# A two-layer hybrid encoder on one core: the latent attention's combine reads PSUM, three TensorE regroupings, the third chunk's weights rounded earlier

## The reference, cut to what matters

```python
def _layer(x, ...):
    h = _rmsnorm(x, g_pre)
    proj = h @ w_in                              # 1024 x 3200, split in columns
    (a_b, a_c, a_h, a_g, b_ql, b_kvl, b_kr, b_g, c_va, c_vb, c_g, d_q, d_k, d_v, d_g) = split(proj)
    ya = a_b * dwconv3(a_c * a_h) * silu(a_g)
    yb = _mla_mixer(b_ql, b_kvl, b_kr, ...) * silu(b_g)
    yc = _conformer_conv_mixer(c_va, c_vb, ...) * silu(c_g)
    yd = _windowed_gqa(d_q, d_k, d_v, ...) * silu(d_g)
    return x + _rmsnorm(concat([ya, yb, yc, yd]) @ w_out, g_post)

def _mla_mixer(q_lat, kv_lat, k_rope, g_q, w_q_up, g_kv, w_kv_up, cos, sin):
    q = _rmsnorm(q_lat, g_q) @ w_q_up            # latent of 192 -> 4 heads x (64 + 32)
    kv = _rmsnorm(kv_lat, g_kv) @ w_kv_up        # latent of 128 -> 4 heads x (64 + 64)
    q_rot, k_rot = _rope(...), _rope(k_rope)
    p = softmax((q_nope k_nope^T + q_rot k_rot^T) * scale)   # over all 1024 keys
    return p @ v

def _conformer_conv_mixer(va, vb, w_dw, b_dw, ln_g, ln_b, w_pw):
    u = dwconv31(va * sigmoid(vb)) + b_dw        # 256 channels
    return silu(layernorm(u)) @ w_pw
```

## Time and profile before

| | |
|---|---|
| time, median of 3 runs | 2278.28 us (2278.1 to 2279.56) |
| the profiled execution's own time | 2278.64 us |
| its span | 2276.9 us |
| mean granted TensorE clock in it | 0.991 of full speed |
| busy: TensorE, VectorE, ScalarE, GpSimd | 2218.9, 1618.6, 1009.5, 534.5 us |

### The profile page before, as it was taken

The page is one execution under the profiler, slowest core; times in us unless marked ns, Lnnn a source line. Parts: engine busy times, 40 slices in busy tenths (PEclk is TensorE's granted clock), DMA queues, the critical chain, the costliest instruction groups (busy, mean ns, idle before and its releaser), DMA issues.

```text
span 2276.9 us, 29336 instructions
## 1 busy us (share of the span) xinstructions
PE 2218.9 (97%) x11506; PEld 1864.7 (82%) x11506; DVE 1618.6 (71%) x2050; ACT 1009.5 (44%) x1795; POOL 534.5 (23%) x312
## 2 busy tenths in 40 slices
PE   7999999999999999999999999999999999999999
PEld 7888887888888888788888888778888888877887
DVE  4499777975459887786445998688653698868853
ACT  4333335863423332686333333367533334336841
POOL 2122223221121222232111222223211212323210
PEclk9999999999999999999999999999999999999999
DMA  5111111034111111003311111100422111110012
GB/s 178 56 38 52 37 38 42 10 102 149 65 65 38 42 38 51 29 15 137 119 62 59 40 49 38 42 28 20 152 108 75 47 38 42 38 42 29 28 65 93
DMA packets 38951, 136.34 MB, mean 60 GB/s; under 512 B 4736, under 2 KB 5248, under 8 KB 38816
## 3 DMA queue, kind: packets, MB, share of 16 engines
q1 hardware_dynamic: 38816, 134.47, 17.3%
HBM read 116.63 MB, written 17.83 MB: 59 GB/s over the span
## 4 chain that ended last, share of the span: by engine, by line
PE 87%; DVE 7%; ACT 3%; issue 1%; DMA 1%; POOL 0%; SPq 0%; DVEq 0%; ACTq 0%
PE ps L536 46%; PE ps L818 14%; PE ps L767 6%; PE ps L802 5%; PE ps L782 4%; PE ps L615 2%; PE ps L641 2%; PE ps L629 2%; PE ps L699 2%; DVE accC L1429 1%; PE ps L546 1%; PE ps L284 1%; DVE PTb L1348 1%; PE ps L744 1%; DVE cat L1641 1%
## 5 line engine op out<-in xcount | busy, mean ns | idle before, releaser
L536 PE MATMUL ps<-hT,stat 128*128 128x512 f32 x4416 | 1061.2, 394 | 3.6 <-POOL stat L894 3.6
L536 PEld LDWEIGHTS ps<-hT,stat 128*128 128x128 f32 x4416 | 819.5, 189 | 168.6 <-POOL stat L894 5.6
L894 POOL TENSOR_TENSOR stat<-raw,stat 128x1024 fp32r<-128x1024 f32 x92 | 250.1, 2718 | 931.0 <-ACT stat L1041 931.0
L1429 DVE SCALAR_TENSOR_TENSOR accC<-uC,parT,accC 128x1024 f32<-128x1024 f32 x240 | 421.3, 1792 | 2.6
L818 PE MATMUL ps<-woR,catR 128*128 128x512 f32 x1488 | 343.3, 391 | 0.1
L818 PEld LDWEIGHTS ps<-woR,catR 128*128 128x128 f32 x1488 | 278.4, 188 | 57.5 <-DVE catR L1348 0.5
L1616 DVE TENSOR_REDUCE bnb<-ps 128x1 f32<-128x1024 f32 x128 | 156.2, 1221 | 44.5 <-PE ps L767 43.9
L1348 DVE TENSOR_TENSOR PTb<-ps,PTb 128x512 fp32r<-128x512 f32 x256 | 163.4, 679 | 18.0 <-ACT PTb L1217 17.1
L1217 ACT ACTIVATE PTb<-ps 128x512 fp32r<-128x512 f32 x256 | 139.0, 595 | 65.3 <-PE ps L782 62.5
L1209 ACT ACTIVATE Pb<-ps,bnb 128x1024 f32<-128x1024 f32 x128 | 143.1, 1118 | 36.4 <-DVE bnb L1616 34.3
L802 PE MATMUL ps<-PTb,Vb 128*128 128x256 f32 x1024 | 159.2, 302 | 0.0
(11 more groups left out here) (201 smaller groups left out, 2866.9 us busy)
## 6 DMA issues: line engine op xcount, KB each, us to landing
raw<-w_in SPq DMA_DIRECT2D x100, 512.0 KB, 3.5
y<-xs SPq DMA_DIRECT2D x31, 512.0 KB, 2.6
raw<-w_out SPq DMA_DIRECT2D x24, 512.0 KB, 3.4
xs<-x SPq DMA_DIRECT2D x16, 512.0 KB, 3.6
xs<-y SPq DMA_DIRECT2D x16, 512.0 KB, 3.6
xd<-x SPq DMA_DIRECT2D x8, 512.0 KB, 8.9
ropeT<-rope SPq DMA_DIRECT2D x4, 1024.0 KB, 5.7
rawX<-w_out SPq DMA_DIRECT2D x8, 512.0 KB, 4.4
```

The lines of the kernel that those rows point to most:

```text
L536: last = mm(ps[:, 2 * (c % 2) + h, cols], w[:, a, k, :], hT[:, h, b, k, cols], start=(k == 0 and (a, b) == (0, 0)), stop=(k == KD - 1 and ...
L894: pool.tensor_tensor(dst[:, 1], src, dst[:, 0].bitcast(F32), ALU.subtract).then_inc(q["wlo"], 1)
L1429: last_tap[j] = conv.add(stt(accC[:, j, :], uC[:, j, t:t + T], w, accC[:, j, :], ALU.mult, ALU.add))
```

## The change

The combine of a pair now has a PSUM operand in each operation: the sum is written back to the bank, the reciprocals are read where they lie, and `rbB` and its copy go. bq1's squares go to a buffer of their own (`aU`), and GpSimd adds them to bq0's, so that there is one round of column sums for the query latent. The mean's two halves are added on VectorE before the product. For the query latent's second block, the lo part is written under the hi part (partitions 64 to 127), and the weights' second block is stored twice, so that one product with 128 rows does hi·hi and hi·lo. Chunk 2's weights are rounded before ScalarE waits for chunk 0. Before its split of the second token block for the output product, GpSimd waits for the last combine.

```diff
-B_SQ = {"bq1": 0, "bkv": 1, "ac1": 2}
+B_SQ = {"bkv": 0, "ac1": 1}
...
# TensorE, chunk dg1
-                            pe.wait_ge(*got("bstat_ok", 3))
-                            pe.wait_ge(*got("conv_ok", 2))
+                            pe.wait_ge(*got("bstat_ok", 2))
+                            pe.wait_ge(*got("msum_ok", 1))
                             for h in range(2):
-                                for j in range(2):
-                                    last = mm(ps[:, 4 + h, :], ones[:, 0:1].broadcast_to([P, P]),
-                                              accC[:, j, h * HALF:(h + 1) * HALF], start=(j == 0), stop=(j == 1))
+                                last = mm(ps[:, 4 + h, :], ones[:, 0:1].broadcast_to([P, P]),
+                                          uC[:, 0, h * HALF:(h + 1) * HALF], start=True, stop=True)
...
                             j = B_SQ[name]
-                            pe.wait_ge(*got("bsq_ok", j + 1))
+                            pe.wait_ge(*(got("bsq_ok", 3) if j else got("bsum_ok", 1)))
                             pe.wait_ge(*got("dm_ok", u + 1))
-                            column_sums(5, 384 + j * NT, aC[0:(P, QR - P, P)[j], :]).then_inc(q["st_b"], 1)
+                            column_sums(5, 384 + j * NT, aC[:, :]).then_inc(q["st_b"], 1)
...
# TensorE, q_up
-                        for kt, rows in ((0, P), (1, QR - P)):
-                            for a, b in three:
+                        for kt, a, b, rows in ((0, 0, 0, P), (0, 0, 1, P), (0, 1, 0, P), (1, 0, 0, P), (1, 1, 0, QR - P)):
...
# GpSimd
                         split_lo(name)
+                        if name == "bkv":
+                            pool.wait_ge(*got("bsq_ok", 2))
+                            pool.tensor_tensor(aC[0:QR - P, :], aC[0:QR - P, :], aU[0:QR - P, :], ALU.add).then_inc(q["bsum_ok"], 1)
...
                     cat_lo(0, slice(2, KD), 2)
+                    pool.wait_ge(*got("bo_ok", NB // 2))
                     cat_lo(1, slice(0, KD), 3)
...
# ScalarE
-                        act.activation(aC[0:rows, :], rawB[0:rows, j, :], ACT.Square).then_inc(q["bsq_ok"], 1)
+                        act.activation((aC, aU, aC)[j][0:rows, :], rawB[0:rows, j, :], ACT.Square).then_inc(q["bsq_ok"], 1)
...
-                        if c + 1 in range(PRE, NC):
+                        if c == 0:
+                            split_hi(CHUNKS[PRE])
+                        if c + 1 in range(PRE + 1, NC):
                             split_hi(CHUNKS[c + 1])
...
-                        act.activation(tmpB[r:r + HD, w % 2, :], b[o:o + HD, 0:256], ACT.Copy)
-                        act.activation(rbB[r:r + HD, w % 2, :], b[r:r + HD, 256:512], ACT.Copy).then_inc(q["bo_tmp"], 1)
+                        act.activation(tmpB[r:r + HD, w % 2, :], b[o:o + HD, 0:256], ACT.Copy).then_inc(q["bo_tmp"], 1)
...
# VectorE, latent_lo
-                        rows, dst = ((P, qlR[:, 0, :, :]), (QR - P, qlR[0:QR - P, 1, :, :]), (P, kvR[:, :, :]))[j]
+                        rows, lo, hi = ((P, qlR[:, 0, 1, :], qlR[:, 0, 0, :]), (QR - P, qlR[QR - P:P, 1, 0, :], qlR[0:QR - P, 1, 0, :]),
+                                        (P, kvR[:, 1, :], kvR[:, 0, :]))[j]
...
                                 ts(accC[:, j, :], accC[:, j, :], 0.5, parT[:, P_CB + j:P_CB + j + 1],
                                    ALU.mult, ALU.add).then_inc(q["conv_ok"], 1)
+                            dve.wait_ge(*got("conv_ok", 2))
+                            tt(uC[:, 0, 0:T], accC[:, 0, :], accC[:, 1, :], ALU.add).then_inc(q["msum_ok"], 1)
...
# VectorE, b_combine
                         b, t = ps[:, 6 + w % 2, :], tmpB[rows, w % 2, :]
-                        own.add(tt(t, b[rows, 0:256], t, ALU.add))
+                        y_ = cat[rows, 2 + h // 2, i * P:(i + 2) * P]
+                        own.add(tt(b[rows, 0:256], b[rows, 0:256], t, ALU.add))
+                        own.add(stt(y_, b[rows, 256:512], 0.5, y_, ALU.mult, ALU.mult))
                         own.wait()
-                        own.add(tt(t, t, rbB[rows, w % 2, :], ALU.mult))
-                        own.wait()
-                        y_ = cat[rows, 2 + h // 2, i * P:(i + 2) * P]
-                        stt(y_, t, 0.5, y_, ALU.mult, ALU.mult).then_inc(q["bo_ok"], 1)
+                        tt(y_, b[rows, 0:256], y_, ALU.mult).then_inc(q["bo_ok"], 1)
...
# host
     wq[:, :QR] = mla_w_q_up[:, :, _q_columns()]
+    wq[:, QR:] = wq[:, P:QR]
```

More of the change, by code:

```diff
@@ L227, in build @@
         crs = sm("crs", NT)
-        bvar = sm("bvar", 3 * NT)
+        bvar = sm("bvar", 2 * NT)
         brs = sm("brs", 2 * NT)
@@ L695, in q_up @@
                         wait_pair(C[name])
-                        for kt, rows in ((0, P), (1, QR - P)):
-                            for a, b in three:
[L698 to L702, removed]
+                        for kt, a, b, rows in ((0, 0, 0, P), (0, 0, 1, P), (0, 1, 0, P), (1, 0, 0, P), (1, 1, 0, QR - P)):
+                            for h in range(2):
+                                last = mm(chunk_ps(name)[:, h * HALF:(h + 1) * HALF], wup[0:rows, a, kt, col:col + P],
+                                          qlR[0:rows, kt, b, h * HALF:(h + 1) * HALF],
+                                          start=((kt, a, b) == (0, 0, 0)), stop=((kt, a) == (1, 1)))
                         last.then_inc(q["ch_done"], 1)
@@ L1487, in latent_lo @@
                     def latent_lo(j):
-                        rows, dst = ((P, qlR[:, 0, :, :]), (QR - P, qlR[0:QR - P, 1, :, :]), (P, kvR[:, :, :]))[j]
+                        rows, lo, hi = ((P, qlR[:, 0, 1, :], qlR[:, 0, 0, :]), (QR - P, qlR[QR - P:P, 1, 0, :], qlR[0:QR - P, 1, 0, :]),
+                                        (P, kvR[:, 1, :], kvR[:, 0, :]))[j]
                         dve.wait_ge(*got("lat_hi", j + 1))
-                        minus(dst[:, 1, :], rawB[0:rows, j, :], dst[:, 0, :]).then_inc(q["lat_lo"], 1)
+                        minus(lo, rawB[0:rows, j, :], hi).then_inc(q["lat_lo"], 1)
                     taps_done = 0
@@ L1518, in _ @@
                             d_recip(u)
-                        if CHUNKS[c] == "bq1":
-                            dve.wait_ge(*got("st_b", 1))
-                            ts(bvar[:, 0:NT], ps[:, 5, 384:384 + NT], 1.0 / QR, EPS, ALU.mult, ALU.add).then_inc(q["bstat_ok"], 1)
-                        if CHUNKS[c] == "bkv":
-                            dve.wait_ge(*got("st_b", 2))
-                            dve.wait_ge(*got("bstat_ok", 1))
-                            stt(bvar[:, 0:NT], ps[:, 5, 384 + NT:384 + 2 * NT], 1.0 / QR, bvar[:, 0:NT], ALU.mult, ALU.add
-                                ).then_inc(q["bstat_ok"], 1)
-                        if CHUNKS[c] == "ac1":
-                            dve.wait_ge(*got("st_b", 3))
-                            ts(bvar[:, 2 * NT:3 * NT], ps[:, 5, 384 + 2 * NT:384 + 3 * NT], 1.0 / KVR, EPS, ALU.mult, ALU.add
-                               ).then_inc(q["bstat_ok"], 1)
+                        if CHUNKS[c] in B_SQ:
+                            j = B_SQ[CHUNKS[c]]
+                            dve.wait_ge(*got("st_b", j + 1))
+                            ts(bvar[:, j * NT:(j + 1) * NT], ps[:, 5, 384 + j * NT:384 + (j + 1) * NT], 1.0 / (QR, KVR)[j], EPS,
+                               ALU.mult, ALU.add).then_inc(q["bstat_ok"], 1)
                         if CHUNKS[c] == "dg0":
```

15 lines of the change are left out of this document (7 added, 8 removed).

## The result

| | before | after |
|---|---|---|
| time, median of 4 runs each, same chip | 2278.92 us (2278.1 to 2280.65) | 2216.93 us (2215.94 to 2217.73) |
| ratio | | 0.9731 (95% interval 0.9719 to 0.9744) |
| the profiled execution, its span | 2278.64, 2276.9 us | 2217.08, 2215.2 us |
| mean granted TensorE clock | 0.991 | 0.999 |

62.0 us faster, 2.7%.

A forecast was written before the change was run, and what follows sets the result against it. TensorE, busy 97% of the span, was taken as the bound. The terms 24.8 + 7.5 + 6.9 + 3.6 + 2.9 - 5.6 + 8 gave 48.1 us, so 2278.3 - 48.1 = 2230 us; range 2219 to 2246.

The forecast's parts named there:

- (h): TensorE's granted clock: five fewer of eleven stretches at clock 0.50, gaining 8 us, bounds 0 and 18.
- (a): Pair combine: with a PSUM input, VectorE operations are no longer held by GpSimd, gaining 24.8 us.
- (b): Pair combine: VectorE writing its sum to PSUM costs 0, at most 0.8 us in all.
- (c): Column sums in the chunks: three blocks of 16 rows become two, gaining 7.5 us, GpSimd's addition hidden.
- (d): Conformer mean: four fp32 products become two, gaining 6.9 us, the added VectorE sum hidden.
- (e): Query up-projection: two of twelve products go; half the saving turns into waiting at L709, leaving 3.6 us.
- (f): Third chunk's weights: waits at L536 for GpSimd go, gaining 2.9 us, 2.1 of it in pass 0.
- (g): Output product: GpSimd's split, waiting for the last combine, delays VectorE's splits; TensorE stalls 1.4 us a pass, costing 5.6.
- Rivals 3, 4 and 5: Combine: PSUM-and-SBUF operations held too, 2258, chance 0.06; PSUM writes far dearer, 2293, chance 0.03; no change, 2278, chance 0.02.
- rival 1: TensorE's clock gives nothing back, as new idle pieces replace the old: 2238 us; no separate chance given.
- Rival 2: Chunk loop: late VectorE turns the column-sum and mean savings into waits, 14.4 us less: 2244 us; chance 0.07.

The follow-up runs named there:

- e1: The kernel before with only the new combine (three operations with a PSUM input, no `rbB` copy): 2239.48 us, ratio 0.983.
- e4: The changed kernel with the three rounds of column sums of before and no GpSimd addition: 2228.28 us, ratio 0.9785.
- e11: The changed kernel with the query's up-projection and lower latent as in the kernel before: 2221.7 us, ratio 0.9755.
- e5: The kernel before, with the second combine operation reading the reciprocals in PSUM and the third still reading SBUF alone: 2264.37 us, ratio 0.9938.
- e6: The kernel before with seven extra TensorE products, results unused, ahead of chunk 2 in pass 0: 2279.75 us.
- e9: The kernel before with its 64-row column sums run over all 128 rows, the upper 64 stale: 2273.48 us, ratio 0.9985.
- e10: The changed kernel with one round of column sums, for the latent keys, covering 64 of the 128 rows: 2222.58 us, ratio 0.976.
- e2: The changed kernel with the old combine and without GpSimd's new wait: 2249.16 us, ratio 0.9876.
- e3: The changed kernel without GpSimd's wait for the last combine ahead of its split: 2212.7 us, ratio 0.9711.
- e7: The changed kernel with seven extra TensorE products, results unused, ahead of chunk 2 in pass 0: 2218.55 us.
- e8: The changed kernel with four extra TensorE products, results unused, ahead of chunk 2 in pass 0: 2218.68 us.
- e12: The changed kernel run once more, unaltered, on another chip: 2217.82 us, ratio 0.9735.

## Why the prediction was wrong, point by point

The failed step is term (h): "I take five fewer in all, 5 x 1.6 = 8". All eleven falls went. At 1.55 each that is 17.1 us, 9.1 more than the term and the greater part of the 13.1 us between 2230 and 2216.93. The price of one was right (1.6 against 1.55), the number was not.

| term | predicted | measured | from |
|---|---|---|---|
| (a), (b) combine | 24.8 | 25.7 | e1's stages, less seven falls |
| (c) column sums | 7.5 | 8.2 | e4's stages |
| (d) mean | 6.9 | 7.4 | 21.8 - 4 x 1.55 - 8.2; e4 in pass 0: 1.86 a pass |
| (e) up-projection | 3.6 | 3.9 | stages; e11 3.9 |
| (f) third chunk | 2.9 | 3.7 | stages; holds 0.6 ahead of the first product |
| (g) GpSimd's wait | -5.6 | -4.4 | output stage 15.8 in e1, 11.4 after |
| (h) clock | 8 | 17.1 | 11 x 1.55 |
| sum | 48.1 | 61.6 | span 61.7 |

**Why (h) was too small.** Two reasons kept six falls in the sum, and both fell. First, the text said that new idle pieces would bring falls of their own, at L709 (now L705) and in the output product. Those pieces are there, shorter than I said (1.27 and 0.86 us against 1.8 and 1.4), and none of them, 32 and 28 in all runs, has a fall behind it.

What keeps them harmless is not shown. Length is the nearest reading: e5 cut place 3 from 3.04 to 2.06 and three of its four falls went. But it is not length alone. In e5 the 1.34 us at place 2, hardly longer than the 1.27 at L705, have a fall in all four passes; there TensorE had stood for another 0.3 us just before (0.72 in the kernel before, so what I called one piece of 1.47 is two, with 1.1 us of work between them). And a piece of one length has a fall in some passes and none in others: 1.46 us at place 2, 1.70 at place 1, 2.79 at chunk 2. What differs there, as far as the traces tell, is the moment at which it comes (e6, e9).

Second, only the eight falls behind idle time were said to go; the three of the chunk loop I kept, since I had no cause for them. They belonged to a block that the change removes. Over all profiled executions of this study, a fall right behind the 64-row sums came in 16 of 24 passes (before 3, e1 1, e4 2, e5 4, e6 3, e10 3), and in none of the 32 passes of the eight kernels with 128-row sums only (after, e2, e3, e7, e8, e9, e11, e12). The two one-line changes, e9 and e10, took the falls away and brought them back. That the 64-row block brings them is shown; what in it does so is not.

**The range.** The size of (h) alone would not have put the time outside: the lower end took (h) at 18, but every other term at its middle, and that is the second fault. The other terms were off by 4.4 us together, all to the same side (0.9 + 0.7 + 0.5 + 0.3 + 0.8 + 1.2). With (h) right, the sum would have given 2278.3 - 57.2 = 2221.1, and the 4.2 below that is the middle terms' own error, for which the lower end had left 2 (18 against 17.1, and the rounding from 2220 to 2219).

**(a), (b)** were right in mechanism, and in size within 0.9 us. The prediction read it from L1636 alone; e5 isolates it. The Trainium skill ("SBUF — State Buffer", Who interferes with whom) says that a VectorE instruction with two SBUF inputs contends with a GpSimd instruction that reads SBUF; by that rule the traces agree, in both directions: held up to 2021 ns with SBUF and SBUF, 431 with PSUM and SBUF. The other page of the Trainium skill that I weighed, "VectorE: DVE Perf Modes" (the errata section), gives a PSUM source 62 cycles more than an SBUF one, an estimated 65 ns; the measurement decides against it for this shape, with 416 to 431 ns in place of 422. Rivals 3, 4 and 5 are out by the same rows, and rival 1 by the eleven falls that went.

**(c), (d)** are both a little over the durations of their rows: 2.05 and 1.85 us a pass against 1.87 and 1.72. What the 0.3 us a pass are was not followed up. Rival 2, that VectorE eats them, is out: the stage gave all of it and more.

**(e)** went as written in kind: about half of the saved products came back as waiting, L705 from 3.1 to 5.1 (I had said about 6.5), and 0.7 in a new wait at L720.

**(f)** was right in kind (the next late thing is VectorE's read of the PSUM pair, the 0.8 us wait for `Qst`) but its size is uncertain: chunk 2 starts between 44.55 and 47.93 us in the nine kernels with that edit and between 48.33 and 48.64 in the five without it, so one execution tells it to no better than a microsecond.

**(g)** was right in mechanism and in the order of things: with T = 479.70, VectorE's split 5 was done at T + 3.1 (I had said 3.3), GpSimd, begun 0.05 us behind it and held by it, at T + 5.35 (5.6), and split 6 at 486.1, T + 6.4 (6.9). The stall was 0.86 and not 1.4, because split 6 ended only 1.08 us behind GpSimd, because all came 0.2 earlier, and because TensorE had work until T + 5.63 and not T + 5.5. In e3 the stall is gone.

## What to carry over

When a change closes idle pieces, list the falls of the clock one by one with what stands ahead of each, and ask for each whether the change removes that thing; a fall with no idle ahead has a cause as well, and a removed block may be it. Put new idle pieces beside old ones by length and by what stands next to them, and take the falls of one execution as one draw: the same piece at another moment may have a fall or none. Where VectorE operations with two SBUF inputs are held by GpSimd, moving one of the two inputs to PSUM was enough here (431 ns against 2324), and a wait that makes GpSimd's work start where VectorE has its own such operations is paid for on the spot (4.4 us). Let the end of a range leave room for all middle terms to be off to the same side.

## What the runs showed of the hardware that I had not expected

- A block of 16 one-column float32 products over 64 rows is followed, with TensorE busy throughout, by 3.4 us at clock 0.50 in 16 of 24 passes; the same block over 128 rows never is, in 32. In the 16, the fall begins 2.3 to 3.4 us after the block does. The Trainium skill ("TensorE: Matmul & The Clock Gate", Why this matters for your kernels) ties throughput drops in mid-kernel to idle time of TensorE; these falls have none ahead of them, so here the measurement goes beyond the page.
- Whether the same work has a fall behind it depends on the moment at which it comes. The 1.5 us of idle time at place 2 of pass 0 had none in the kernel before and one in e6, where it ended 0.35 us earlier. The 1.7 us at place 1 had none in the kernel before and one in three passes of e9, where they ended 0.8 to 1.7 us earlier. By what rule the moment counts was not worked out.
- A VectorE operation of 64x256 that writes PSUM costs 15 ns more at the median than one that writes SBUF (431 against 416 ns).
